# Attention in-projection of a hybrid encoder: half of its contraction computed as 2x2 block products, seven in place of eight

## What is computed

```
h = x * (1 + scale) + shift                       # adaLN, from c @ ada_w + ada_b
proj = h @ w_in                                   # 1024 x 1024 by 1024 x 10240
q, k, v of three groups (window, dilation) in ((128,1), (512,4), (2048,16)); gate
o_g = softmax(q k^T / 8 - slope * distance) v     # inside the window, for each group
o = sum over groups, weighted by the softmax of the groups' log-denominators
y = (o * silu(gate)) @ w_out
x = LN(alpha * x + gate_ada * y) * g + b
```

## Time and profile before

| | us |
|---|---|
| median of 3 executions | 2168.78 |
| lowest, highest | 2166.26, 2169.51 |
| span of the profiled execution | 2173.1 |
| TensorE busy | 2074.4 (95%) |
| VectorE busy | 1051.4 (48%) |
| ScalarE busy | 963.3 (44%) |
| GpSimd busy | 826.5 (38%) |

### The profile page before, as it was taken

The page is one execution under the profiler, slowest core; times in us unless marked ns, Lnnn a source line. Parts: engine busy times, 40 slices in busy tenths (PEclk is TensorE's granted clock), DMA queues, the critical chain, the costliest instruction groups (busy, mean ns, idle before and its releaser), DMA issues.

```text
span 2173.1 us, 32149 instructions
## 1 busy us (share of the span) xinstructions
PE 2074.4 (95%) x11075; PEld 1653.5 (76%) x11075; DVE 1051.4 (48%) x2381; ACT 963.3 (44%) x2357; POOL 826.5 (38%) x436
## 2 busy tenths in 40 slices
PE   5999999999999999999999989899999999998997
PEld 4787887888878878878877777677777777776886
DVE  5522323223232233222333477788488488488553
ACT  3333433334334343333334345575475475485320
POOL 1211141221411413214114182476376375386472
PEclk9999999999999999999999999999999999999998
DMA  8412121221212212112221341655365265367431
GB/s 294 136 40 69 42 84 50 60 68 40 68 66 56 73 39 70 63 35 68 68 67 43 111 151 43 146 164 159 101 173 157 95 175 146 100 198 229 169 117 39
DMA packets 106242, 221.19 MB, mean 102 GB/s; under 512 B 18979, under 2 KB 53411, under 8 KB 105637
## 3 DMA queue, kind: packets, MB, share of 16 engines
q1 hardware_dynamic: 106148, 219.98, 33.6%
HBM read 195.75 MB, written 24.19 MB: 101 GB/s over the span
## 4 chain that ended last, share of the span: by engine, by line
PE 73%; DVE 10%; issue 5%; POOL 4%; ACT 4%; DMA 3%; SPq 1%; DVEq 0%; ACTq 0%; POOLq 0%
PE pp L535 39%; PE pp_s L2036 8%; PE tp L567 4%; PE sp_ L557 4%; PE yo_p L2240 3%; PE op L640 2%; PE pp_s L2240 2%; DVE stage_s L2666 2%; DMA w_raw_s<-in_b_w 2%; DVE vv L2602 2%; PE st_p L2240 1%; PE fill L2240 1%; PE op L629 1%; POOL trunk L1945 1%; PE tp L576 1%
## 5 line engine op out<-in xcount | busy, mean ns | idle before, releaser
L467 POOL TENSOR_TENSOR w_lo<-w_raw,w_hi 128x1024 fp32r<-128x1024 f32 x79 | 191.0, 2418 | 833.9 <-ACT w_hi L813 833.9
L535 PE MATMUL pp<-h_hi,w_hi 128*128 128x512 f32 x1232 | 488.6, 397 | 0.0
L535 PE MATMUL pp<-h_hi,w_lo 128*128 128x512 f32 x1232 | 480.3, 390 | 0.0
L535 PE MATMUL pp<-h_lo,w_hi 128*128 128x512 f32 x1232 | 479.7, 389 | 0.0
L1091 DVE COPY probT<-tp 128x512 f32<-128x512 f32 x160 | 103.2, 686 | 544.6 <-PE tp L567 544.6
L2036 PE MATMUL pp_s<-h_hi,w_hi_s 128*128 128x512 f32 x624 | 268.8, 431 | 20.4 <-DVE stage_s L2666 14.3
L535 PEld LDWEIGHTS pp<-h_hi,w_hi 128*128 128x128 f32 x1232 | 231.4, 188 | 49.4 <-issue 4.3
L535 PEld LDWEIGHTS pp<-h_hi,w_lo 128*128 128x128 f32 x1232 | 231.2, 188 | 49.5
L535 PEld LDWEIGHTS pp<-h_lo,w_hi 128*128 128x128 f32 x1232 | 231.6, 188 | 45.5
L874 ACT ACTIVATE prob<-prob,mz 128x256 f32<-128x256 f32 (+2 forms) x384 | 170.4, 446 | 191.7 <-DVE mz L1071 191.7
L2036 PE MATMUL pp_s<-h_hi,w_lo_s 128*128 128x512 f32 x624 | 245.8, 394 | 1.9 <-issue 1.9
(11 more groups left out here) (458 smaller groups left out, 3606.6 us busy)
## 6 DMA issues: line engine op xcount, KB each, us to landing
w_raw<-in_a_w SPq DMA_DIRECT2D x80, 512.0 KB, 3.3
rw<-cum_rows SPq DMA_DIRECT2D x32, 1024.0 KB, 6.3
w_raw_s<-in_b_w SPq DMA_DIRECT2D x40, 512.0 KB, 4.0
ew<-exp_rows SPq DMA_DIRECT2D x64, 256.0 KB, 7.3
num_wide<-in_ada_w SPq DMA_DIRECT2D x16, 768.0 KB, 6.5
num_wide<-merge_rows SPq DMA_DIRECT2D x16, 768.0 KB, 7.8
num_wide<-in_ada_w SPq DMA_DIRECT2D x20, 512.0 KB, 6.2
yT_b<-trunk SPq DMA_DIRECT2D x32, 256.0 KB, 2.4
```

Source lines behind the costliest of these rows:

```text
L467: nc.gpsimd.tensor_tensor(lo.rearrange("p k c -> p (k c)"), w_raw[:, slot].rearrange("p k c -> p (k c)"), hi.rearrange("p k c -> p (k c)") ...
L535: last = nc.tensor.matmul(pp[:, par, :], w[:, slot, k, :], keep[h][:, k, half * HALF:(half + 1) * HALF], start=(k == 0 and n == 0), stop=( ...
```

## The change

Two tiles of weights and the two token halves are treated as a 2x2 block product over one half of the contraction (4 of the 8 contraction tiles, as two blocks of `KS` = 2). Eight block products become seven with sums of blocks: four sums of h blocks (S1 to S4) are made once, three sums of weight blocks (t2, t3, t4) for each pair of tiles (a "duo"), and nine additions of 128x512 bring the products together. The other four contraction tiles (`PL`) are multiplied as before ("plain").

- TensorE: a duo has `first_half` (even step: 48 matmuls) and `second_half` (odd step: 42), in place of 4 x 24. Three banks b0, b1, b2 hold the products; one bank is left for the values (`op`), in place of two.
- VectorE: `first_sums` (four operations) and `second_sums` (five) in each duo, on PSUM and two SBUF buffers ua, va. In step 5 of the loop some weighings of the next modulation, in step 7 half of the gate, stand inside `second_sums`; in step 9 the first part of `shares`.
- GpSimd: makes the differences of weight blocks (in place in `w_raw`, and into `t_raw`) and the remainders of `w_raw` and of t2, t3, t4 (`early`, `late`). Before the loop it makes the sums of h blocks.
- ScalarE: rounds both weight slots, t2 and t3 together, t4; before the loop the sums of h. In step 1 the numerators of step 0 are copied after the evacuations, no longer before the softmax.
- Memory: h and its sums lie over `trunk`, so x^T is loaded into four small buffers; y of each pair goes to memory from `wide[:, 1]` (`store_y`) and comes back in the last pair (`load_y`, eight loads). The gate vector of the modulation is formed as columns by eight small matmuls in place of four of width 512 and one row addition, and TensorE waits once for `n_set` before the loop.
- Order: before the loop three tiles, then one plain tile, then one duo; the loop has five duos a pair, (VT2, Q2), (K2, VT0), (Q0, K0), (GATE, VT1), (Q1, K1); the last pair has two, in steps 0 to 3, and its output products begin in step 6. The gate rows' loads after the second now stand on SP behind the load of the first duo, which waits for the fourth tile's remainder.

```diff
+KS = 2
+PL = KT - 2 * KS
+A11, A12, A22, S1, S2, S3, S4 = range(7)
+DUOS_OF_TILES = ((VT2, Q2), (K2, VT0), (Q0, K0), (GATE, VT1), (Q1, K1))
+LAST_DUOS = ((VT2, Q2), (K2, GATE))
+FIRST_DUO = (Q1, K1)
+PLAIN = 4
+NT_UNITS = 1 + 5 * (PAIRS - 1) + 2
+EVENTS, SUMS = 9, 9
...
+                def passes(bank, weights, hs_, begin, end):
+                    (w1, w2), (h1, h2) = weights, hs_
+                    for i, (w, h) in enumerate(((w1, h1), (w1, h2), (w2, h1))):
+                        last = nc.tensor.matmul(bank, w, h, start=begin and i == 0, stop=end and i == 2)
+                    return last
+                def product(bank, weights, form, begin=False, end=False):
+                    for i in range(KS):
+                        last = passes(bank, [w[:, i, :] for w in weights], [h[:, form, i, :] for h in hs],
+                                      begin and i == 0, end and i == KS - 1)
+                    return last
+                def plain(bank, slot, half, begin=False, end=False):
+                    for k in range(PL):
+                        last = passes(bank, [w[:, slot, k, :] for w in (w_hi, w_lo)], [h_of(i, k, half) for i in range(2)],
+                                      begin and k == 0, end and k == PL - 1)
+                    return last
+                def rows_of(slot, rows):
+                    return [w[:, slot, rows, :] for w in (w_hi, w_lo)]
+                B_X, B_Y = slice(PL, PL + KS), slice(PL + KS, KT)
+                T2, T3 = ([t_hi[:, i], t_lo[:, i]] for i in range(2))
+                T4 = [t4_hi, t_lo[:, 2]]
+                def first_half(n):
+                    first = isinstance(n, int) and n == 0
+                    pe.wait_ge(w_ready, 4 * n + 1)
+                    pe.wait_ge(pp_free, PP_FREE + 4 * n - 1)
+                    product(b0, rows_of(0, B_X), A11, begin=True, end=True).then_inc(pp_full, 1)
+                    if first:
+                        pe.wait_ge(pp_free, PP_FREE)
+                    product(b1, rows_of(0, B_Y), A12, begin=True)
+                    plain(b1, 0, 0, end=True).then_inc(pp_full, 1)
+                    pe.wait_ge(w_ready, 4 * n + 2)
+                    pe.wait_ge(pp_free, PP_FREE + 4 * n)
+                    if first:
+                        pe.wait_ge(h_lo, KT + 1)
+                    product(b2, T2, S2, begin=True, end=True).then_inc(pp_full, 1)
+                    pe.wait_ge(comb, SUMS * n + 1)
+                    if first:
+                        pe.wait_ge(h_lo, KT + 2)
+                    product(b0, T3, S3, begin=True, end=True).then_inc(pp_full, 1)
+                    pe.wait_ge(comb, SUMS * n + 3)
+                    plain(b2, 0, 1, begin=True).then_inc(pp_full, 1)
+                def second_half(n, between=None):
+                    pe.wait_ge(w_ready, 4 * n + 4)
+                    product(b2, T4, A22, end=True).then_inc(pp_full, 1)
+                    pe.wait_ge(pp_free, PP_FREE + 4 * n + 1)
+                    if isinstance(n, int) and n == 0:
+                        pe.wait_ge(h_lo, KT + 4)
+                    product(b1, rows_of(1, B_X), S1, begin=True, end=True).then_inc(pp_full, 1)
+                    pe.wait_ge(comb, SUMS * n + 4)
+                    plain(b0, 1, 1, begin=True, end=True).then_inc(pp_full, 1)
+                    if between:
+                        between()
+                    pe.wait_ge(pp_free, PP_FREE + 4 * n + 2)
+                    product(b2, rows_of(1, B_Y), S4, begin=True)
+                    plain(b2, 1, 0, end=True).then_inc(pp_full, 1)
...
+                def early(n):
+                    pool.wait_ge(w_in[0], 16 * n + 48)
+                    pool.wait_ge(w_in[1], 16 * n + 48)
+                    if not isinstance(n, int) or n:
+                        pool.wait_ge(pp_full, PP_FULL + EVENTS * n - EVENTS + 4)
+                    t2, t3 = (t_raw[:, i] for i in range(2))
+                    nc.gpsimd.tensor_tensor(t3, w_raw[:, 1, B_Y, :], w_raw[:, 1, B_X, :], ALU.subtract)
+                    link(n, nc.gpsimd.tensor_tensor(w_raw[:, 1, B_X, :], w_raw[:, 1, B_X, :], w_raw[:, 0, B_X, :],
+                                                    ALU.subtract), 1)
+                    nc.gpsimd.tensor_tensor(t2, w_raw[:, 1, B_Y, :], w_raw[:, 1, B_X, :], ALU.subtract
+                                            ).then_inc(t_made, 1)
+                    pool.wait_ge(w_rounded, 4 * n + 1)
+                    rest(w_lo[:, 0], w_raw[:, 0], w_hi[:, 0]).then_inc(w_ready, 1)
+                    pool.wait_ge(w_ready, 4 * n + 1)
+                    link(n, nc.gpsimd.tensor_tensor(w_raw[:, 0, B_Y, :], w_raw[:, 0, B_Y, :], w_raw[:, 1, B_Y, :],
+                                                    ALU.subtract), 2)
+                    pool.wait_ge(w_rounded, 4 * n + 2)
+                    rest(t_lo[:, 0:2], t_raw[:, 0:2], t_hi[:]).then_inc(w_ready, 1)
+                def late(n):
+                    pool.wait_ge(w_rounded, 4 * n + 3)
+                    rest(w_lo[:, 1], w_raw[:, 1], w_hi[:, 1]).then_inc(w_ready, 1)
+                    if not isinstance(n, int) or n:
+                        pool.wait_ge(pp_full, PP_FULL + EVENTS * n)
+                    nc.gpsimd.tensor_tensor(t_raw[:, 2], w_raw[:, 0, B_Y, :], w_raw[:, 1, B_X, :],
+                                            ALU.add).then_inc(t_made, 1)
+                    pool.wait_ge(w_rounded, 4 * n + 4)
+                    link(n, rest(t_lo[:, 2], t_raw[:, 2], t4_hi), 3)
+                    pool.sem_inc(w_ready, 1)
...
+                def first_sums(n):
+                    dve.wait_ge(pp_full, PP_FULL + EVENTS * n + 1)
+                    if not isinstance(n, int) or n:
+                        dve.wait_ge(comb, SUMS * n)
+                    nc.vector.tensor_copy(ua, b0).then_inc(comb, 1)
+                    dve.wait_ge(pp_full, PP_FULL + EVENTS * n + 2)
+                    dve.wait_ge(comb, SUMS * n + 1)
+                    nc.vector.tensor_tensor(b1, b1, ua, ALU.add).then_inc(comb, 1)
+                    dve.wait_ge(pp_full, PP_FULL + EVENTS * n + 3)
+                    dve.wait_ge(comb, SUMS * n + 2)
+                    nc.vector.tensor_tensor(ua, b2, ua, ALU.add).then_inc(comb, 1)
+                    dve.wait_ge(pp_full, PP_FULL + EVENTS * n + 4)
+                    dve.wait_ge(comb, SUMS * n + 3)
+                    nc.vector.tensor_tensor(va, b0, ua, ALU.add).then_inc(comb, 1)
+                def second_sums(n, beside=None, before_last=None):
+                    dve.wait_ge(pp_full, PP_FULL + EVENTS * n + 6)
+                    dve.wait_ge(comb, SUMS * n + 4)
+                    nc.vector.tensor_tensor(b2, b2, va, ALU.add).then_inc(comb, 1)
+                    dve.wait_ge(pp_full, PP_FULL + EVENTS * n + 7)
+                    dve.wait_ge(comb, SUMS * n + 5)
+                    nc.vector.tensor_tensor(va, b1, va, ALU.add).then_inc(comb, 1)
+                    nc.vector.tensor_tensor(ua, b1, ua, ALU.add).then_inc(comb, 1)
+                    if beside:
+                        beside()
+                    dve.wait_ge(pp_full, PP_FULL + EVENTS * n + 8)
+                    dve.wait_ge(comb, SUMS * n + 6)
+                    nc.vector.tensor_tensor(b0, b0, va, ALU.add).then_inc(comb, 1)
+                    if before_last:
+                        before_last()
+                    dve.wait_ge(pp_full, PP_FULL + EVENTS * n + 9)
+                    dve.wait_ge(comb, SUMS * n + 7)
+                    nc.vector.tensor_tensor(b2, b2, ua, ALU.add).then_inc(comb, 1)
...
+                def begin_pair(j, before, kinds):
+                    second_tile(j - 1 if before else j, 5 * j, DUOS_OF_TILES[4] if before else FIRST_DUO, 0)
+                    if before:
+                        nc.scalar.activation(qscale[:], qscale[:], ACT.Copy, scale=2.0).then_inc(scale_set, 1)
+                        act.wait_ge(scale_set, j)
+                    round_r2(5 * j + 1)
+                    if before:
+                        numerators(j - 1, DUOS - 1)
+                    round_t4(5 * j + 1)
+                    softmax(j, 2)
+                    softmax(j, 3)
+                    first_tile(j, 5 * j + 1, kinds, 0)
...
                 with act.Fori(0, PAIRS - 1) as j:
                     for d in range(1, DUOS):
-                        unit(j, 2 * d - 1, STEP_TILES, T_AT)
-                        weights_at(j, d + 1)
-                        numerators(j, d - 1)
+                        n = 5 * j + (d // 2 + 1)
+                        kinds = DUOS_OF_TILES[d // 2]
+                        if d % 2:
+                            round_r1(n + 1)
+                            if d > 1:
+                                numerators(j, d - 1)
+                        else:
+                            second_tile(j, n - 1, DUOS_OF_TILES[d // 2 - 1], 0)
+                            round_r2(n)
+                            numerators(j, d - 1)
+                            round_t4(n)
```

(37 more changed lines are left out.)

618 lines of the change are left out of this document (383 added, 235 removed).

## The result

The changed kernel takes 2150.9 us (median, 2147.0 to 2158.7) against 2168.8 (2165.9 to 2171.1): ratio 0.992, 95% interval 0.9896 to 0.9945. A second set of runs gave 2153.2 against 2170.4, ratio 0.9914 (0.9897 to 0.993). The forecast was 2132, which is a ratio of 0.983. Its range (2116 to 2160) holds the time, but the gain is 17 to 18 us instead of 36.8. The mechanism is there; something gives half of it back. The profiled executions are single ones: the first of the changed kernel took 2158.7 us, the longest of its five, and the second 2153.5, close to its median.

What follows compares the result with a forecast made beforehand. TensorE, busy 95% of the span, was taken as the bound; -51.7 +7.4 +3.5 +1.5 +2.5 = -36.8 from the span of 2173.1 gave 2136.3, and carrying over 4.3 gave 2132 us, range 2116 to 2160.

Steps and rivals of the forecast that it cites:

- The price of a matmul, -51.7: All 38 duos: 6 matmuls fewer in each, at 0.227 us from the distance of starts, -51.7 us.
- Sums: VectorE in each duo: nine additions of 128x512 at 0.7 us, 6.3 us in some 26.
- The gate bank, +7.4: Step 7: ScalarE empties the gate's bank after eight exponentials, so TensorE waits 1.05 us a pair, seven looped pairs, +7.4.
- Numerators and the one output bank, +3.5: Start of step 2: values of step 1 wait for the numerators' copy, 0.5 us in each of seven pairs, +3.5.
- Before the loop, +1.5, between -1 and +8: Head: fewer matmuls, against 2 to 3 us waiting for the first sum and 1 us for the modulation's columns; net +1.5.
- rival (e): Clock drops from bank waits: 2.3 us each, one a duo gives 87 us, 2219; slower from 16 duos; chance 0.07.
- The last pair, +2.5: Last pair: output products a step later, y returns in eight loads, ScalarE 1 us behind; +2.5, between -3 and +10.
- The carry-over, -4.3: Whole program: the median of the runs is 4.3 us below the profiled span of 2173.1, carried over to the forecast.
- (a): All waits hidden, ScalarE and GpSimd half a microsecond earlier than forecast: 2117 us, chance 0.12.
- (b): Hand-overs bite in most duos, with sums at 1.34 us: 1 us a duo, 38 instead of 10.9, 2159; chance 0.14.
- (c): Head or tail collide, at the upper bounds of their terms: +14 us, 2146, chance 0.08.

Runs made afterwards that it cites:

- both edits: Changed kernel with gate rows 0 to 3 weighed ahead of the value copies and loads of rows 2 to 5 issued ahead of SyncE's wait: 2141.2 us.
- either edit alone: Changed kernel with two gate rows weighed ahead of the value copies: 2150.9 us; with only loads of rows 2 to 5 ahead of SyncE's wait: 2152.4 us.

## Why the forecast missed, step by step

- **The price of a matmul, -51.7.** Right: 51.3 to 53.5 by putting them back. 0.227 from the distances held, and the pair without waits came to 136.42.
- **Sums.** Right: 0.68 to 0.70 us for a copy or an addition, with the result in PSUM too (line 1367: 700 ns, 38 times; like all of them it has one operand in PSUM and one, `ua` or `va`, in SBUF). VectorE has room for them in the loop.
- **The gate bank, +7.4.** Right in place and size (0.73 idle for 1.05; 1.03 a pair in time, 7.2 in all).
- **Numerators and the one output bank, +3.5.** Too high. The pair with the gate's wait removed has no idle time at all, so this costs 0. The path was read rightly and is tight: in the pair at 552.89 the numerators' copy ends at 576.64 us and the values of step 1 start at 576.74, with no idle time of TensorE before them. The forecast had the copy end 0.4 us too late for them.
- **Before the loop, +1.5, between -1 and +8.** This is the step that failed. The head lost 17.4 us in the profiled run (15.3 to 15.9 of them behind the small sum), far over the upper bound, and 3 more in the first pair. The working itself adds up to 1.6 to 2.6, not 1.5, but five parts of it were wrong. It had the loads of rows 2 to 7 come 12 us later, and then let VectorE follow them at its old pace; but it left the two value copies out of VectorE's queue. The change puts them ahead of the weighings (a part of the edit that the cut above leaves out), and they hold VectorE until 81.8. With only two slots for the rows that delay goes back into the loads. The experiments show these two together: both undone give 9.7 us. The rest is read from the trace. It took the remainders at 1.2 us; in the mean of the four they are 2.1. It took the gate's column sums at 0.5 us; the eight of them (line 844) took 1.84, as much as the row's 1.88 had. It did not see that TensorE waits for the next layer's weighings, which now stand between two of VectorE's sums (1.3 us; the wait of 0.7 for the columns behind them was in its 1 us). So the first sum came at 109.0 and not at about 98, while TensorE wanted it at 98.8. And it priced no half speed behind the wait, which is the next point.

```
-                for k in range(KT):
-                    dve.wait_ge(g_in[k % 2], 16 * (k // 2 + 1))
-                    weigh_rows(k, g_acc, g_ring[k % 2], g_used)
                 for at in range(2):
                     copy_t(("v", at // 2, at % 2), at, at % 2)
...
+                weigh_gate(range(4))
```

- **The clock.** Held to be a cause of loss only as rival (e), slower. In the loop it stays at 1.00 under waits of 0.73 us, 47 of them in seven profiles. But it falls during the head's single long wait, and the forecast priced 2 to 3 us of waiting there without it. That took 2.9 us. The second stretch, 3.4 us, stays in kernels without the long wait (6.8 us at half speed from 117.7 on with both edits), and is halved where the next layer's weighings are moved; what sets the rest of it is open.
- **The last pair, +2.5.** The last part is 1054.2 and 1056.7 us, which makes the term 4.3 and 6.8, inside -3 to +10; the kernels of the study spread from 1052.0 to 1056.7 in this part, so it is measured no closer. No experiment touched it.
- **The carry-over, -4.3.** It is the distance of a median from one execution that happened to be profiled. The executions of this study have a time 1.8 us above their span, so the profiled one of before took about 2174.9 us (an estimate), 6 above its median; for the changed kernel the distance is 6.0 in the first profile, and 1.5 the other way in the second.
- **Rivals.** (a) would have needed a hidden gate bank; (b), hand-overs in most duos, is ruled out by a pair with one wait in it. What happened is (c), the collision in the head, over its bound: 2146 forecast, 2151 found. It had 0.08, too little for a head whose queues had all been reordered.

The Trainium skill, Perfetto Trace Analysis, section Matmuls, has groups rotate through banks so that emptying one is hidden. By that rule the one bank in each odd step would show; here one step of ten did, and it was mended by the order of ScalarE, with no bank more.

## What to carry to other kernels

When an edit frees the bounding engine in a loop, walk the prologue with the same care, instruction by instruction on every queue that was reordered: two copies that wait, placed ahead of work that had been free to start, and loads placed behind a wait cost more here (9.7 us) than all the new waits of the loop (7.2). A ring shared by a loading queue and a working queue has to be moved on both sides; either edit alone measured as nothing in the medians, and a test that takes back one of them would have cleared both. Compare profiles from a mark just ahead of the edit: here that took out 4 us of scatter and let an effect of 2 us be seen. Price a wait of several microseconds on TensorE with the half-speed stretch that follows it.
